# Latent norm moved to the linear recurrence's end, decay stages regrouped, third attention gate projection moved ahead of the second pair's softmax

## What is computed

```python
h = rmsnorm(x, norm_gain);  proj = h @ w_in        # gq gk gv gb ga gz | mq mkv mkr mz | lx lz
qkv = silu(causal_dwconv([gq, gk, gv]))            # q, k are l2-normed, 4 heads of 128
o_a = gated_delta_rule(q, k, v, g, beta)           # triangular solves inside chunks
o_a = rmsnorm(o_a) * silu(gz)
qm = rmsnorm(mq) @ mla_w_uq                        # latent norm: mq 384, mkv 256 features
kv = rmsnorm(mkv) @ mla_w_ukv
o_b = causal_attention(qm, kv, rope) * silu(mz)    # 8 heads, in 4 pairs
o_c = rg_lru(causal_dwconv(lx)) * silu(lz)         # linear recurrence (scan over tokens)
x = x + concat(o_a, o_b, o_c) @ w_out
```

## Time and profile before

| | us |
|---|---|
| median of 3 runs | 1642.65 |
| lowest and highest | 1640.84, 1644.35 |
| the profiled execution | 1642.59 |
| its span | 1640.8 |

### The profile page before, as it was taken

The page is one execution under the profiler, slowest core; times in us unless marked ns, Lnnn a source line. Parts: engine busy times, 40 slices in busy tenths (PEclk is TensorE's granted clock), DMA queues, the critical chain, the costliest instruction groups (busy, mean ns, idle before and its releaser), DMA issues.

```text
span 1640.8 us, 24598 instructions
## 1 busy us (share of the span) xinstructions
PE 1569.6 (96%) x10174; PEld 1359.6 (83%) x10174; DVE 1029.2 (63%) x1599; ACT 893.3 (54%) x1419; POOL 65.0 (4%) x58
## 2 busy tenths in 40 slices
PE   7989999998989999999989999989999999899999
PEld 7989877998877788889977888878888888678887
DVE  6877675796766755545785655456555556765454
ACT  5986464686565545446446544445454456654442
POOL 0013000011200000000000000000000000000000
PEclk9999999999999999999999999999999999999999
DMA  7624224542413666555423556544665553246552
GB/s 231 204 71 144 78 102 137 180 143 72 154 53 121 200 207 196 186 180 165 146 91 107 188 186 199 180 130 154 205 200 182 184 163 120 78 156 197 186 183 100
DMA packets 203616, 252.55 MB, mean 154 GB/s; under 512 B 17136, under 2 KB 183280, under 8 KB 203376
## 3 DMA queue, kind: packets, MB, share of 16 engines
q1 hardware_dynamic: 203504, 250.97, 47.7%
HBM read 249.90 MB, written 1.05 MB: 153 GB/s over the span
## 4 chain that ended last, share of the span: by engine, by line
PE 78%; DVE 11%; ACT 7%; issue 2%; DMA 1%; SPq 0%; POOL 0%; DVEq 0%; ACTq 0%; POOLq 0%
PE bank L802 75%; ACT arena L1487 4%; DVE weights_rest L2039 3%; DVE arena L2187 2%; ACT weights_high L1487 1%; PE bank L1250 1%; DMA ring<-in_w_in 1%; ACT L1482 1%; ACT L1487 1%; DVE xT_rest L2433 1%; DVE small L2361 0%; PE bank L1184 0%; PE bank L859 0%; DVE x L2402 0%; DVE weights_rest_more L2039 0%
## 5 line engine op out<-in xcount | busy, mean ns | idle before, releaser
L2039 DVE TENSOR_TENSOR weights_rest<-ring,weights_high 128x1024 fp32r<-128x1024 f32 (+2 forms) x410 | 474.0, 1200 | 173.0 <-ACT weights_high L1487 171.1
L1487 ACT ACTIVATE weights_high<-ring 128x1024 fp32r<-128x1024 f32 (+2 forms) x410 | 398.7, 1026 | 133.8 <-PE bank L802 116.8
L802 PE MATMUL bank<-weights_high,xT_high 128*128 128x512 f32 (+1 forms) x864 | 330.5, 387 | 8.8 <-DVE xT_rest L2433 3.5
L802 PE MATMUL bank<-weights_high,xT_rest 128*128 128x512 f32 (+1 forms) x800 | 301.5, 377 | 0.0
L1487 ACT ACTIVATE arena<-bank 128x512 f32<-128x512 f32 (+5 forms) x316 | 142.9, 471 | 266.6 <-PE bank L802 256.8
L802 PE MATMUL bank<-xT_high,weights_high 128*128 128x256 f32 (+1 forms) x936 | 275.2, 294 | 4.7 <-DVE xT_rest L2133 2.4
L802 PE MATMUL bank<-xT_rest,weights_high 128*128 128x256 f32 (+1 forms) x936 | 268.2, 287 | 0.0
L802 PE MATMUL bank<-xT_high,weights_rest 128*128 128x256 f32 (+1 forms) x904 | 258.8, 286 | 0.0
L802 PE MATMUL bank<-weights_rest,xT_high 128*128 128x512 f32 (+1 forms) x680 | 256.4, 381 | 0.0
L802 PEld LDWEIGHTS bank<-weights_high,xT_high 128*128 128x128 f32 x864 | 162.4, 189 | 42.0 <-issue 5.0
L802 PEld LDWEIGHTS bank<-xT_high,weights_high 128*128 128x128 f32 (+1 forms) x936 | 181.6, 194 | 10.2 <-issue 4.6
(11 more groups left out here) (187 smaller groups left out, 1956.7 us busy)
## 6 DMA issues: line engine op xcount, KB each, us to landing
ring<-in_w_in SPq DMA_DIRECT2D x36, 1024.0 KB, 5.3
ring<-in_ffn_w_gate SPq DMA_DIRECT2D x71, 512.0 KB, 4.0
ring<-in_ffn_w_up SPq DMA_DIRECT2D x71, 512.0 KB, 5.0
ring<-in_ffn_w_down SPq DMA_DIRECT2D x34, 1024.0 KB, 4.9
ring<-in_w_out SPq DMA_DIRECT2D x22, 1024.0 KB, 4.9
ring<-in_w_in_a SPq DMA_DIRECT2D x11, 1024.0 KB, 5.3
ring_more<-in_ffn_w_down SPq DMA_DIRECT2D x10, 1024.0 KB, 5.0
ring_more<-in_ffn_w_gate SPq DMA_DIRECT2D x17, 512.0 KB, 4.0
```

The lines of the kernel that those rows point to most:

```text
L802: return eng.matmul(o, a, b, start=first, stop=last)
L1487: return eng.activation(dst, src, func, **kw_)
L2039: TTs(rest_slot(b)[:, part], raw_slot(b)[:, part], high_slot(key)[:, part].bitcast(F32), ALU.subtract).then_inc(*dv.mark(("rest", key, z)))
```

## The change

It edits the list of stages in three places and the waits of two stages on ACT.

- `mla_norm` goes from behind `silu` 2 to right behind `lru_c`, in front of the projection gk 1. Its ACT stage no longer waits for `l2`'s products of q and k; instead `l2` 0 on ACT waits for the latent products on DVE (`mla32`), as the buffer `rn` is now used in the other order.
- `decay` goes from behind `silu` 1 to in front of the projection gv 0; `decay_b` from behind gv 1 to in front of it.
- The gate projection `mz` 2 goes from behind `sm` 1 to in front of `att` 1. On PE that is in front of `pv` 0, as the scores of pair 1 (`sc` 1) come earlier in the list.

```diff
-        out += [proj("gq", 1), ("lru_b", l), proj("mkv"), ("silu", l, 0), proj("gk", 0), ("lru_c", l)]
-        out += [proj("gk", 1), ("l2", l, 0), proj("gv", 0), ("silu", l, 1), ("decay", l), proj("lz", 0), proj("gv", 1)]
-        out += [("decay_b", l), ("l2", l, 1), proj("lz", 1), ("silu", l, 2), ("mla_norm", l), proj("gz", 0), ("vT", l)]
+        out += [proj("gq", 1), ("lru_b", l), proj("mkv"), ("silu", l, 0), proj("gk", 0), ("lru_c", l), ("mla_norm", l)]
+        out += [proj("gk", 1), ("l2", l, 0), ("decay", l), proj("gv", 0), ("silu", l, 1), proj("lz", 0), ("decay_b", l), proj("gv", 1)]
+        out += [("l2", l, 1), proj("lz", 1), ("silu", l, 2), proj("gz", 0), ("vT", l)]
...
-        out += [("sc", m, 1), ("gdn_w", l), ("gdn_n", l, 0), ("att", m, 1), ("pv", m, 0), ("gdn_o", l, 1), ("sm", m, 1)]
-        out += [proj("mz", 2), ("gdn_n", l, 1), ("parts", f"h{l}", "c", "a")]
+        out += [("sc", m, 1), ("gdn_w", l), ("gdn_n", l, 0), proj("mz", 2), ("att", m, 1), ("pv", m, 0), ("gdn_o", l, 1), ("sm", m, 1)]
+        out += [("gdn_n", l, 1), ("parts", f"h{l}", "c", "a")]
...
                     g = ("l2", l, p)
                     ac.wait_ge(*at(g))
-                    if p >= 2:
-                        ac.wait_ge(*at(("qk", l, p - 2)))
+                    ac.wait_ge(*at(("qk", l, p - 2) if p >= 2 else ("mla32", l, 1)))
...
                 g = ("mn", l)
                 ac.wait_ge(*at(g))
-                ac.wait_ge(*at(("qk", l, 2)))
-                ac.wait_ge(*at(("qk", l, 3)))
```

## The result

The changed kernel takes 1626.44 us (median of 4 runs, 1623.23 to 1628.02) beside 1642.98 (1640.84 to 1644.35): ratio 0.9899, 95% interval 0.9887 to 0.9911, 16.5 us less. The profiled execution took 1628.02 us, its span is 1626.2.

The account below looks back on a forecast made before the run. TensorE was taken as the bound, with only its idle and low-clock time to win. Gains of 7.0 (layer 0), 7.8 (layer 1) and 3.5 us (mz 2's move) sum to 18.3: 1624.3 us, likeliest 1617 to 1631, 8 in 10 1615 to 1635.

Follow-up runs that it names:

- norm_split: The changed kernel with the norm's two ACT copies and the subtractions that follow in a task of their own behind gk 1; 1623.52 us, ratio 0.9889.
- rows128: The changed kernel with decay_b's 16 products contracting over all 128 rows of the tile instead of 4; 1625.22 us, ratio 0.9894.
- decayb_back: The changed kernel with decay_b put back behind gv 1; 1632.44 us, ratio 0.9938.

## What to carry to other kernels

A step moved off the end of one engine's queue lands in front of everything behind it there; it pays when another edit makes the same time free ahead of the next thing due, and two such edits are worth nothing like their sum (2.0 and 4.6 us alone, 13.1 together). Move with it in thought what its helpers on other engines do: the squares on POOL gave back 2.7 us of DVE where they left (the convolutions of gv 0, 6.46 to 3.75) and took 1.4 where they arrived, but there ACT, and in layer 1 TensorE, stood and waited for them. And before removing a stall of TensorE, look for what would be late a microsecond later: norm_split took the norm's wait away, and silu 2 ended only 0.7 us earlier; rows128 took the fall away and put 1.62 us of products in its place.

## What the hardware did that I had not expected

- The granted clock can fall without an idle gap. Behind 16 products that use 4 of 128 rows, between two projections, it was 0.50 for 3.4 us with PE busy at 1.00, in 10 of 12 layers (in one of the ten PE had waited 1.31 us just before the products); with dense products among them or in their place, in none of 8.
- A product of 256 columns over 4 rows takes 0.12 us (1.99 for 16), the same over 128 rows 0.23 (3.61 for 16), both at full clock.
- Four weight halves on DVE took 8.44 us beside 6.73 us of POOL's products, for some 4.7 by the pairs of 2.35 without it: 3.7 us lost in 6.7, more than half of POOL's time. The Trainium skill (SBUF — State Buffer, its part on the shared port pair) has an exclusive lock for the whole POOL instruction, by which, as an estimate, up to 6.7 us would be lost; the row shows less. Six convolution steps beside 1.3 us of POOL take 3.75 us, where they took 6.46 beside 4.6.
- A wait of TensorE can cost more than its length: in decayb_back v's transposes of layer 0 come 1.9 us later than in the changed kernel (111.86 against 109.95), behind a wait of 2.65 us, and with the clock at 0.50 for 3.4 us behind it the first pt comes 3.7 us later (190.31 against 186.65). With the wait of 2.63 us in layer 1 added, the whole kernel is 6.4 us slower.
